# Modulation products inside the attentions, issued as two rounds of four matmuls

## The chip, the cores and the metric

The kernel runs on one core of a Trainium2 chip. The metric is the device time of one execution, in microseconds (us). Three runs of the kernel before gave 1478.65, 1478.90 and 1479.46, median 1478.9.

## The reference

Two trunk layers run over 128 context tokens and 256 latent tokens with a model width of 1024. A layer is: an adaptively modulated RMSNorm, one input projection, three parallel mixers (A: differential attention over 4 heads, B: pooling, C: windowed attention over 8 heads with a sink), a gated merge, an output projection, again a modulated norm, and a channel mixer (dense in layer 0, top-2-of-8 experts in layer 1).

What matters here is where the modulation comes from. `adaln_mods` computes six vectors per layer from a conditioning vector: `m = silu(c) @ w_ada[l] + b_ada[l]`, with `w_ada[l]` of 1024 x 6144. There are two conditioning vectors, one for latent and one for context tokens. So two rows are multiplied with 25 MB of weights a layer. The result is needed only at the norms and residuals of the rest of the layer and of the next, so the kernel computes it in pieces, placed among other work.

## The kernel before, in words

All 384 tokens are kept together as three blocks of 128. TensorE (PE) is the engine with the most work. Large products run in three passes of split operands (`mm3`, lines 766 to 768); the stages inside the attentions run as plain fp32 matmuls.

**The weights' path.** SyncE's queue (SP) loads every weight slot of 1 MB, as two transfers of 512 KB (`halves`, line 517), into a ring of three buffers (`raw`). Slot n goes to buffer n mod 3, and SP waits until the last user of that buffer is done. Slots that belong to `w_ada` need no splitting: PE reads `raw` itself, and when the product of a slot is complete PE raises `mm_done`, which lets SP refill the buffer.

**A modulation slot** covers 256 columns of `w_ada` and all 1024 rows (8 chunks k of 128). `ada_product` waits for both transfers of the slot, and then issues 8 matmuls with 32 stationary columns each. Matmul k goes to column group k mod 4 of the array and adds to the 32 PSUM partitions of that group in bank 7, so four matmuls can run beside each other, and a product is two rounds of four. The profile counts 2 instructions for a matmul: a product is 16 instructions of line 783, a round is 8.

**The attentions.** `attention(l, kind)` runs four times on PE: A and then C in layer 0 (phases 2 and 3), A and C in layer 1 (phases 4 and 5). Each walks 12 steps t, one for a head or a pair of heads (t // 3) and a block of queries (t % 3); block 0 has 128 keys, the others 384. In step t PE issues in this order, and PE keeps to its order:

- `scores(t + 2)`, the score matmuls of two steps ahead (line 1004), for t from 2 to 9;
- a modulation product, if t is in `ADA_STEPS`;
- `transposes(t)`, the turn of the weights (line 1022), which waits until VectorE (DVE) has combined the exponentials (`p_done`);
- `values(t - 1)` (line 1038), which waits for ScalarE's (ACT) copy of the turned weights.

For a step, the other engines do: DVE the maxima (line 2233), ACT two exponentials (line 1721), DVE the combination (lines 2244 or 2248), and, after the turn, ACT a copy to SBUF (line 1732). ACT's order is exps(t + 1), copy(t), with exps(11) behind copy(9). The DVE of attention C also has a sum of 1.75 us in step 5 (line 2288).

**Modulation slots.** The phases have 8, 7, 6 and 6 slots. Products 0 and 1 come ahead of step 0; the others stand in the steps named. When the attention begins, slots 0 to 2 are in the three buffers. Slot 3 can be loaded only when product 0 has been computed, slot 4 after product 1, slot 5 after product 2, and so on.

```
ADA_STEPS = {2: (1, 3, 5, 7, 9, 10), 3: (1, 4, 6, 8, 10),
             4: (1, 4, 6, 9), 5: (1, 4, 6, 9)}
for t in range(12):
    if t >= 2 and t + 2 < 12:
        scores(l, kind, t + 2)
    if t in ADA_STEPS[phase]:
        ada_product(phase, 2 + ADA_STEPS[phase].index(t))
    transposes(t)
    if t >= 1:
        values(t - 1)
```

Outside the attentions the same kind of product appears at line 793 (`gap_product`): one product alone, and later five in a row.

Of the kernel before, what the change touches and what calls it, by code (L numbers as in the profile page):

```python
# [15 lines left out]
KD = D // P  # L16
# [49 lines left out]
ADA_SLOTS = (8, 4, 8, 7, 6, 6)  # L66
# [10 lines left out]
EARLY_BUF = {0: 0, 1: 1, 2: 2, 3: 3, 4: 4, 5: 0, 7: 1, 9: 2}  # L77
EARLY = 5
GROUPS = ADA_SLOTS[0] // 2
ADA_STEPS = {2: (1, 3, 5, 7, 9, 10), 3: (1, 4, 6, 8, 10), 4: (1, 4, 6, 9), 5: (1, 4, 6, 9)}  # L80
assert all(2 + len(ADA_STEPS[p]) == ADA_SLOTS[p] <= 16 for p in ADA_STEPS)
SQS = (0, 1, 1 + N_HALF, 2 + N_HALF)
SQ0 = (0, BLK, BLK + 5 * N_HALF, BLK + 5 + 5 * N_HALF)
PROJ = ((0, 512), (512, 512), (2048, 512), (2560, 256), (1024, 512), (1536, 512))
# [55 lines left out]
def prefix_step_kernel(nc, a, outs, const):  # L140
    y_prompt, y_sample, new_dk, new_dv, new_wk, new_wv = outs
    ctx = ExitStack()
    with ctx:
# [12 lines left out]
        def sem(name):  # L156
            return ctx.enter_context(nc.semaphore(name))
# [162 lines left out]
        hi_done, lo_done, mm_done = sem("hi_done"), sem("lo_done"), sem("mm_done")  # L320
# [77 lines left out]
        def ada_slot(phase, i):  # L398

            if phase == 0:  # L400
                return FIRST_ADA[i]
            if phase == 1:
                return ADA_SLOTS[0] + 3 + RING * i
            l, kind = (phase - 2) // 2, (phase - 2) % 2
            return gate_slot(l, kind + 1, 0, 0) - ADA_SLOTS[phase] + i
# [17 lines left out]
        def ada_raw(n):  # L423

            return early[:, EARLY_BUF[n], :] if n in EARLY_BUF else raw[:, n % RING, :]
# [43 lines left out]
        def weight_col(t):  # L469

            return 1 + (T - P if t % 3 == 0 and t else 0)
# [24 lines left out]
        def raw_wait(eng, n, more=0):  # L496
            if n in EARLY_BUF:
                eng.wait_ge(side_in[EARLY_BUF[n]], early_wait(n))
            else:
                eng.wait_ge(raw_in[n % RING], more + 32 * raw_turn(n))  # L500
# [262 lines left out]
        def _(pe):  # L763
# [7 lines left out]

                return [w[:, n % RING, :].rearrange("p (k c) -> p k c", k=k) for w in (whi, wlo)]

            def ada_product(phase, i):

                n, last, bank = ada_slot(phase, i), ADA_SLOTS[phase] - 1, 7
                if phase == 0:
                    i, last = i % 2, 1
                raw_wait(pe, n)
                w = ada_raw(n).rearrange("p (k c) -> p k c", k=KD)  # L780
                for k in range(KD):
                    j = k % 4
                    mm = pe.matmul(ps[32 * j:32 * j + 32, bank, 0:256], sil32[:, k, 30 - 2 * i:62 - 2 * i], w[:, k, :],  # L783
                                   start=(i == 0 and k < 4), stop=(i == last and k >= 4), tile_position=(0, 32 * j))
                mm.then_inc(mm_done, 1)

            def gap_product(phase, i):
                last = GAP_SLOTS[phase] - 1
# [8 lines left out]
            def ada_pair(g):  # L797
                if g:
                    pe.wait_ge(ada_read, g)
                for i in range(2 * g, 2 * g + 2):  # L800
                    ada_product(0, i)

            def ada_end(phase, g=0):
                n = 2 * (GAP_SLOTS[phase] if phase in GAP_SLOTS else ADA_SLOTS[phase]) if phase else 4
                pe.wait_ge(ada_row, ada_turn(phase) if phase else g + 1)
                for c in range(2):
                    mm = pe.matmul(ps[:, 7, 256 + 32 * c:256 + 32 * c + n], adarow[:, c * P:(c + 1) * P], pick[:, 0:n],
                                   start=True, stop=True)
                mm.then_inc(ada_turned, 1)
# [52 lines left out]
            def first_units(products):  # L862
# [25 lines left out]
                for b in range(BLK):  # L888
                    if b == 2:
                        ada_product(0, 6)  # L890
                    mm = pair(K_A, 1, b)
                mm.then_inc(mm_done, 1)
                ada_product(0, 7)
                ada_end(0, 3)
                pe.wait_ge(lo_done, split_count(win_slot(0, 1) + 1))
# [97 lines left out]
            def scores(l, kind, t):  # L993

                h, qb = t // 3, t % 3
                if t >= 2:
                    pe.wait_ge(e_done, 24 * l + 12 * kind + t - 1)
                nk, k0 = (P, 0) if qb == 0 else (T, P)
                q, kk = (qTA, kTA[:, h, k0:k0 + nk]) if kind == 0 else (qTC, kTC[:, h // 2, k0:k0 + nk])
                for m in range(2):  # L1000
                    r = slice(64 * m, 64 * m + 64)
                    c0 = score_col(t) if kind else 0
                    out, lhs = ps[:, 2 * (t % 2) + m, c0:c0 + nk], q[r, h, qb * P:(qb + 1) * P]
                    mm = pe.matmul(out, lhs, kk[r], start=True, stop=True)  # L1004
                mm.then_inc(s_done, 1)

            def attention(l, kind):

                st0 = 24 * l + 12 * kind
                it0 = 24 * l + 12 * kind  # L1010
                phase = 2 + 2 * l + kind

                def transposes(t):
                    pe.wait_ge(p_done, st0 + t + 1)
                    if kind:
                        pe.wait_ge(pt_evac, it0 + t)
                    elif it0 + t >= 2:
                        pe.wait_ge(pt_evac, it0 + max(t - 1, 0))
                    k0 = kind * weight_col(t)
                    for m in range(1 + kind):  # L1020
                        for kb in range(1 if t % 3 == 0 else 3):
                            mm = pe.transpose(ps[:, 4 + (m if kind else t % 2), kb * P:(kb + 1) * P],  # L1022
                                              ebuf[:, t % 2, m, k0 + kb * P:k0 + (kb + 1) * P], ident)
                    mm.then_inc(tp_done, 1)

                def values(t):
                    h, qb = t // 3, t % 3
                    pe.wait_ge(pt_evac, it0 + t + 1)
                    grp = 8 * l + 4 * kind + h
                    if qb == 0 and grp >= 1:  # L1030
                        pe.wait_ge(o_evac, grp)
                    c = slice(h * P, (h + 1) * P) if kind == 0 else slice(512 + (h // 2) * 64, 576 + (h // 2) * 64)
                    keys = [vtok[:, 0, c]] if qb == 0 else [vtok[:, 1, c], vtok[:, 2, c], ctxv[:, c]]
                    for kb, v in enumerate(keys):
                        k = slice(kb * P, (kb + 1) * P)
                        for m in range(1 + kind):
                            rows, x = (slice(64 * m, 64 * m + 64), ptm[:, t % 2, m, k]) if kind else (slice(0, P), pt[:, t % 2, k])
                            mm = pe.matmul(ps[rows, 6, qb * P:(qb + 1) * P], v, x, start=(kb == 0),  # L1038
                                           stop=(kb == len(keys) - 1))
                    mm.then_inc(pv_done, 1)  # L1040

                scores(l, kind, 2)
                scores(l, kind, 3)
                pe.wait_ge(merge_top, 2 * l + kind + 1)
                ada_product(phase, 0)
                ada_product(phase, 1)
                if kind == 0:
                    pe.wait_ge(merge_done, 6 * l + 2)
                else:
                    pe.wait_ge(merge_read, 4 * l + 2)  # L1050
                for t in range(12):
                    if t >= 2 and t + 2 < 12:
                        scores(l, kind, t + 2)
                    if t in ADA_STEPS[phase]:
                        ada_product(phase, 2 + ADA_STEPS[phase].index(t))
                    transposes(t)
                    if t >= 1:
                        values(t - 1)
                    if t == 11 and kind == 1:
                        ada_end(phase)  # L1060
                values(11)
# [435 lines left out]
            for b in range(BLK):  # L1497
                pe.wait_ge(x_in[b], 16)
                for k in range(KD):
                    mm = pe.transpose(ps[:, 2 * b + k // 4, k % 4 * P:(k % 4 + 1) * P], xtok[:, b, k * P:(k + 1) * P], ident)  # L1500
                mm.then_inc(x_tr, 1)
                if b == 0:
                    pe.wait_ge(init_in, 16 * n_init)
                    for l in range(DEPTH):
                        n = R_END if l == 0 else R_C
                        mm = pe.transpose(ps[:, 6, l * P:l * P + n], vrows[0:n, l, :], ident[0:n, 0:n])
# [11 lines left out]
            for l in range(DEPTH):  # L1518
                if l:
                    mean_squares(2 * l)  # L1520
                input_projection(l)
                branch(l, 0)
                attention(l, 0)
                branch(l, 1)
                attention(l, 1)
                branch(l, 2)
                out_projection(l)
                if l == 0:
                    mean_squares(1)
                    units()  # L1530
                else:
                    router()
                    experts()
# [1240 lines left out]
```

## Time and profile before

| what | value |
|---|---|
| median of three runs | 1478.9 us |
| time of the profiled execution | 1479.42 us |
| span of the profiled execution | 1477.7 us |
| PE busy | 1445.6 us (98%) |
| DVE, ACT busy | 907.6 us (61%), 729.4 us (49%) |
| mean granted clock | 0.998 |
| attention A / C of layer 0 | 26.9 us / 32.1 us |
| attention A / C of layer 1 | 25.5 us / 31.3 us |

The span is from the first to the last instruction. The time is 1.7 us more than the span. The four attentions are 115.8 us of it together. The ends of matmuls in the trace are modelled, so the distance from one start to the next start is the safer measure of what a group of matmuls costs PE.

### The profile page before, as it was taken

What the parts mean: (1) busy time and instruction counts of PE and PEld (TensorE: products, weight loads), DVE (VectorE), ACT (ScalarE), POOL (GpSimd) and SP (SyncE); (2) the same over time, 40 slices, a digit from 0 to 9 for tenths busy, and PEclk for the clock granted to TensorE, in tenths of its full rate; (3) what the DMA queues carried; (4) which work ended last, traced back from release to release, by engine and by line L of the source; (5) the groups of instructions that cost most, each with busy time, mean ns of one, the idle gap of its engine ahead of it and who ended that gap; (6) DMA issues with size and microseconds to landing.
All of it is one profiled execution on the core that took longest, in us unless ns stands there. A gap on an engine that the chain in (4) does not pass through costs nothing.

```text
span 1477.7 us, 22390 instructions
## 1 busy us (share of the span) xinstructions
PE 1445.6 (98%) x8951; PEld 1276.5 (86%) x8951; DVE 907.6 (61%) x1081; ACT 729.4 (49%) x867; POOL 59.7 (4%) x59
## 2 busy tenths in 40 slices
PE   7999999999999999999999999999999999999997
PEld 5788969789999999998889879699888888888884
DVE  4543266555644345427532373737899999989888
ACT  4433354453433233225434262733478787787754
POOL 0100000000000000001000000001200000000030
PEclk9999999999999999999999999999999999999999
DMA  9844365468763355263532271645599999999991
GB/s 325 287 162 165 114 209 183 130 203 276 235 198 108 115 143 142 95 233 125 172 126 86 94 244 62 215 156 194 172 390 395 390 391 394 391 388 383 350 330 65
DMA packets 229146, 326.48 MB, mean 221 GB/s; under 512 B 8485, under 2 KB 154822, under 8 KB 228798
## 3 DMA queue, kind: packets, MB, share of 16 engines
q1 hardware_dynamic: 220160, 296.02, 58.7%
q0 software_dynamic: 6832, 25.88, 5.0%
q10 hardware_dynamic: 2062, 3.24, 0.6%
q8 instruction: 71, 1.16, 0.3%
q14 instruction: 21, 0.17, 0.0%
HBM read 310.14 MB, written 14.97 MB: 220 GB/s over the span
## 4 chain that ended last, share of the span: by engine, by line
PE 91%; DVE 4%; DMA 2%; ACT 1%; issue 1%; ACTq 0%; POOL 0%; DVEq 0%; SPq 0%; POOLq 0%
PE ps L766 26%; PE ps L768 25%; PE ps L767 25%; PE ps L783 2%; PE ps L1004 2%; PE ps L1038 1%; PE ps L1022 1%; DMA mrows<-g2d 1%; DMA raw<-in_w_ex_down_dram 1%; PE ps L859 1%; PE ps L1326 1%; PE ps L1286 1%; PE ps L983 0%; ACT ebuf L1721 0%; PE ps L793 0%
## 5 line engine op out<-in xcount | busy, mean ns | idle before, releaser
L766 PE MATMUL ps<-hhi,whi 128*128 128x384 f32 x824 | 277.0, 336 | 0.3 <-DVE hidlo L2659 0.3
L768 PE MATMUL ps<-hhi,wlo 128*128 128x384 f32 x824 | 275.7, 335 | 0.0
L767 PE MATMUL ps<-hlo,whi 128*128 128x384 f32 x824 | 275.7, 335 | 0.0
L2047 DVE TENSOR_TENSOR wlo<-raw,whi 128x2048 fp32r<-128x2048 f32 x65 | 148.7, 2289 | 173.7 <-ACT whi L1549 161.6
L766 PEld LDWEIGHTS ps<-hhi,whi 128*128 128x128 f32 x824 | 154.8, 188 | 2.6 <-issue 2.0
L767 PEld LDWEIGHTS ps<-hlo,whi 128*128 128x128 f32 x824 | 154.8, 188 | 0.3
L768 PEld LDWEIGHTS ps<-hhi,wlo 128*128 128x128 f32 x824 | 154.8, 188 | 0.0
L2538 DVE TENSOR_TENSOR wlo<-mraw,whi 128x2048 fp32r<-128x2048 f32 (+2 forms) x72 | 143.5, 1993 | 14.4 <-ACT whi L1818 14.0
L2538 DVE TENSOR_TENSOR wlo<-raw,whi 128x2048 fp32r<-128x2048 f32 (+2 forms) x72 | 144.3, 2019 | 11.9 <-ACT whi L1818 11.6
L1549 ACT ACTIVATE whi<-raw 128x2048 fp32r<-128x2048 f32 x60 | 114.6, 1912 | 74.0 <-PE ps L768 58.9
L1818 ACT ACTIVATE whi<-mraw 128x2048 fp32r<-128x2048 f32 (+2 forms) x72 | 120.9, 1679 | 57.1 <-PE ps L768 54.7
L766 PE MATMUL ps<-whi,xgh 128*128 128x512 f32 (+1 forms) x384 | 146.2, 381 | 0.3 <-DVE xgl L2527 0.3
L768 PE MATMUL ps<-whi,xgl 128*128 128x512 f32 (+1 forms) x384 | 142.9, 372 | 0.0
L767 PE MATMUL ps<-wlo,xgh 128*128 128x512 f32 (+1 forms) x384 | 142.9, 372 | 0.0
L1818 ACT ACTIVATE whi<-raw 128x2048 fp32r<-128x2048 f32 (+2 forms) x72 | 121.6, 1698 | 32.9 <-PE ps L768 24.6
L766 PE MATMUL ps<-whi,hhi 128*128 128x512 f32 (+1 forms) x285 | 108.9, 382 | 3.3 <-issue 2.0
L2645 DVE TENSOR_TENSOR wlo<-raw,whi 128x2048 fp32r<-128x2048 f32 (+1 forms) x35 | 73.8, 2109 | 57.9 <-ACT whi L1795 57.9
L768 PE MATMUL ps<-whi,hlo 128*128 128x512 f32 (+1 forms) x285 | 106.2, 372 | 0.0
L767 PE MATMUL ps<-wlo,hhi 128*128 128x512 f32 (+1 forms) x285 | 106.1, 372 | 0.0
L1795 ACT ACTIVATE whi<-raw 128x2048 fp32r<-128x2048 f32 (+1 forms) x36 | 63.8, 1771 | 54.4 <-PE ps L768 54.4
L766 PEld LDWEIGHTS ps<-whi,xgh 128*128 128x128 f32 x384 | 72.2, 188 | 12.5 <-issue 2.0
L768 PEld LDWEIGHTS ps<-whi,xgl 128*128 128x128 f32 x384 | 72.2, 188 | 10.2
(422 smaller groups left out, 2500.2 us busy)
## 6 DMA issues: line engine op xcount, KB each, us to landing
raw<-in_w_ada_dram SPq DMA_DIRECT2D x62, 512.0 KB, 5.3
raw<-in_w_gate_dram SPq DMA_DIRECT2D x48, 512.0 KB, 4.6
raw<-in_w_ex_up_dram SPq DMA_DIRECT2D x24, 1024.0 KB, 8.9
raw<-in_w_ex_down_dram SPq DMA_DIRECT2D x24, 1024.0 KB, 8.4
raw<-in_w_in_dram SPq DMA_DIRECT2D x43, 512.0 KB, 5.7
raw<-in_w_ex_gate_dram SPq DMA_DIRECT2D x16, 1024.0 KB, 8.1
mraw<-in_w_ex_gate_dram SPq DMA_DIRECT2D x16, 1024.0 KB
mraw<-in_w_ex_down_dram SPq DMA_DIRECT2D x16, 1024.0 KB, 9.4
```

Source lines behind the costliest of these rows:

```text
L766: pe.matmul(out, s[0], m[0], start=first, stop=False, **kw)
L767: pe.matmul(out, s[0], m[1], start=False, stop=False, **kw)
L768: return pe.matmul(out, s[1], m[0], start=False, stop=last, **kw)
L783: mm = pe.matmul(ps[32 * j:32 * j + 32, bank, 0:256], sil32[:, k, 30 - 2 * i:62 - 2 * i], w[:, k, :], start=(i == 0 and k < 4), stop=(i == ...
L859: mm = pe.transpose(ps[:, bank, b * P:(b + 1) * P], src, ident)
L1004: mm = pe.matmul(out, lhs, kk[r], start=True, stop=True)
L1549: act.activation(whi[:, n % RING, :], raw[:, n % RING, :], copy).then_inc(hi_done, 1)
L1795: act.activation(whi[:, s % RING, 0:used], raw[:, s % RING, 0:used], copy).then_inc(hi_done, 1)
L1818: act.activation(whi[:, m % RING, c:E_USED[m]], mraw[m % MRAW][:, c:E_USED[m]], copy).then_inc(hi_done, 1)
L2047: dve.tensor_tensor(wlo[:, n % RING, :], raw[:, n % RING, :], whi[:, n % RING, :].bitcast(F32), ALU.subtract).then_inc(lo_done, 1)
L2538: dve.tensor_tensor(wlo[:, m % RING, c:E_USED[m]], mraw[m % MRAW][:, c:E_USED[m]], whi[:, m % RING, c:E_USED[m]].bitcast(F32), ALU.subtrac ...
L2645: dve.tensor_tensor(wlo[:, s % RING, 0:used], raw[:, s % RING, 0:used], whi[:, s % RING, 0:used].bitcast(F32), ALU.subtract).then_inc(lo_d ...
```

## The change

`ada_product` gets an argument for the chunks k that it issues, and raises `mm_done` only with the last chunk. The table of steps is replaced by a table of halves: entry n of `ADA_HALVES[phase]` is the step in which half n is issued, and half n is round n % 2 of product 2 + n // 2. In every step the first half named stands where the product stood, ahead of the turn; a second one (only step 4 of phase 2) stands behind the turn. The wait for the slot's transfers is made before each half, and is for both transfers.

```diff
-ADA_STEPS = {2: (1, 3, 5, 7, 9, 10), 3: (1, 4, 6, 8, 10), 4: (1, 4, 6, 9), 5: (1, 4, 6, 9)}
+ADA_HALVES = {2: (0, 1, 2, 3, 4, 4, 5, 6, 7, 8, 9, 10), 3: (1, 2, 3, 4, 5, 6, 7, 8, 9, 10), 4: (1, 2, 4, 5, 6, 7, 9, 10), 5: (1, 2, 4, 5, 6, 7, 9, 10)}
...
-            def ada_product(phase, i):
+            def ada_product(phase, i, ks=range(KD)):
...
-                for k in range(KD):
+                for k in ks:
...
-                mm.then_inc(mm_done, 1)
+                if ks[-1] == KD - 1:
+                    mm.then_inc(mm_done, 1)
...
+                def ada_half(n):
+                    ada_product(phase, 2 + n // 2, range(4 * (n % 2), 4 * (n % 2) + 4))
...
-                    if t in ADA_STEPS[phase]:
-                        ada_product(phase, 2 + ADA_STEPS[phase].index(t))
+                    halves = [n for n, step in enumerate(ADA_HALVES[phase]) if step == t]
+                    if halves:
+                        ada_half(halves[0])
                     transposes(t)
+                    for n in halves[1:]:
+                        ada_half(n)
```

## Rows read from the trace of the kernel before

**Rows 1.** The page, part 4: shares of the chain that ended last, by engine.
```profile
PE 91%; DVE 4%; DMA 2%; ACT 1%; issue 1%; ACTq 0%; POOL 0%; DVEq 0%; SPq 0%; POOLq 0%
```

**Rows 2.** Busy time by stretch, the four attentions: stretch, length, engines, clock, DMA share, GB/s.
```profile
194.10:221.00 26.90, 26.38 (x254) 16.29 (x253) 19.52 (x46) 16.83 (x54) 0.00 (x0) 1.00 0.87 280
275.60:307.70 32.10, 30.58 (x325) 18.45 (x324) 21.85 (x50) 20.97 (x58) 0.00 (x0) 1.00 0.70 230
841.00:866.50 25.50, 24.53 (x220) 15.43 (x220) 19.52 (x46) 16.92 (x54) 0.00 (x0) 1.00 0.78 247
921.10:952.40 31.30, 29.72 (x310) 18.07 (x309) 22.05 (x51) 21.41 (x58) 0.00 (x0) 1.00 0.64 202
```

**Rows 3.** Timeline of PE, attention A of layer 0: start, us, engine, line, operation.
```profile
199.09 0.92 PE L1004 MATMUL ps<-kTA,qTA 64*128 64x384 f32 x4
200.05 0.55 PE L1022 MATMUL ps<-cst,ebuf 128*128 128x128 f32 x3
...
202.04 1.07 PE L783 MATMUL ps<-raw,sil 128*32 128x256 f32 x16
203.05 0.33 PE L1022 MATMUL ps<-cst,ebuf 128*128 128x128 f32 x1
...
204.40 0.55 PE L1022 MATMUL ps<-cst,ebuf 128*128 128x128 f32 x3
...
206.02 1.07 PE L783 MATMUL ps<-raw,sil 128*32 128x256 f32 x16
...
214.07 0.92 PE L1004 MATMUL ps<-kTA,qTA 64*128 64x384 f32 x4
214.92 1.07 PE L783 MATMUL ps<-raw,sil 128*32 128x256 f32 x16
215.92 0.33 PE L1022 MATMUL ps<-cst,ebuf 128*128 128x128 f32 x1
...
218.84 0.55 PE L1022 MATMUL ps<-cst,ebuf 128*128 128x128 f32 x3 [0.23 <-DVE ebuf L2244]
...
220.30 0.71 PE L1038 MATMUL ps<-pt,vtok 128*128 128x128 f32 x4 [0.24 <-ACT pt L1732]
...
220.99 0.42 PE L1095 MATMUL ps<-hhi,whi 128*128 128x384 f32 x1
```

**Rows 4.** Timeline of SP: second transfers of slots 3, 4 and 5, phase 2.
```profile
196.80 0.51 SPq L517 DMA_DIRECT2D raw<-in_w_ada_dram  x1
197.90 0.51 SPq L517 DMA_DIRECT2D raw<-in_w_ada_dram  x1
199.26 1.20 SPq L517 DMA_DIRECT2D raw<-in_w_ada_dram  x1
```

**Rows 5.** Line 517 by itself, the same three issues in order: time to landing.
```profile
DMA to landing us min/median/max: 4.6/4.6/4.6
...
DMA to landing us min/median/max: 8.0/8.0/8.0
...
DMA to landing us min/median/max: 9.6/9.6/9.6
```

**Rows 6.** The chain in order of time: one modulation product, then five in a row.
```profile
393.79 1.00 PE ps L793 x16
...
395.65 4.45 PE ps L793 x80
```

**Rows 7.** Timeline of ACT: the exponentials of step 11, phases 2 and 3.
```profile
216.46 0.57 ACT L1721 ACTIVATE ebuf<-ps,small 128x384 f32<-128x384 f32 x1
...
302.03 0.58 ACT L1721 ACTIVATE ebuf<-ps,small 128x385 f32<-128x385 f32 x1 [0.72 <-DVE small L2233]
```

**Rows 8.** Timeline of PE: waits for DVE in phases 3, 4 and 5.
```profile
289.73 0.87 PE L1022 MATMUL ps<-cst,ebuf 128*128 128x128 f32 x6 [0.63 <-DVE ebuf L2248]
...
864.72 0.55 PE L1022 MATMUL ps<-cst,ebuf 128*128 128x128 f32 x3 [0.73 <-DVE ebuf L2244]
...
935.28 0.87 PE L1022 MATMUL ps<-cst,ebuf 128*128 128x128 f32 x6 [0.62 <-DVE ebuf L2248]
```

More of the change, by code:

```diff
@@ L79 @@
 GROUPS = ADA_SLOTS[0] // 2
-ADA_STEPS = {2: (1, 3, 5, 7, 9, 10), 3: (1, 4, 6, 8, 10), 4: (1, 4, 6, 9), 5: (1, 4, 6, 9)}
-assert all(2 + len(ADA_STEPS[p]) == ADA_SLOTS[p] <= 16 for p in ADA_STEPS)
+ADA_HALVES = {2: (0, 1, 2, 3, 4, 4, 5, 6, 7, 8, 9, 10), 3: (1, 2, 3, 4, 5, 6, 7, 8, 9, 10), 4: (1, 2, 4, 5, 6, 7, 9, 10), 5: (1, 2, 4, 5, 6, 7, 9, 10)}
+assert all(4 + len(ADA_HALVES[p]) == 2 * ADA_SLOTS[p] <= 32 and max(ADA_HALVES[p]) < 11 for p in ADA_HALVES)
 SQS = (0, 1, 1 + N_HALF, 2 + N_HALF)
```

## The prediction

> **What bounds the kernel now.** I read the chain of waits first: PE holds 91% of it [rows 1], so anything that makes PE's own sequence longer or shorter shows in the time nearly one for one. Then the busy time by stretch, for the four attentions that the change touches. There PE is busy for 26.38 of 26.90, 30.58 of 32.10, 24.53 of 25.50 and 29.72 of 31.30 us [rows 2]. The idle time is the difference, 0.5 + 1.5 + 1.0 + 1.6 = 4.6 us. This is the most that a better filling of PE's waits could ever give, 0.3% of the time, and a change that only moves rounds can fill a part of it. The rest is small print: where the waits lie, what the rounds cost, and whether their weights are there. For the weights I read SP's timeline with its times to landing. In the first attention DMA is busy for 87% of the stretch at 280 GB/s [rows 2], so this is the one of the four in which weights can be late. The list of PE's waits names none between the attentions and up to the router, so what one gains or loses is not given back there.
>
> **The price of a round.** The number of matmuls stays the same. One product alone takes 1.00 us; five in a row take 4.45 [rows 6]. With p for a product and s for what a group costs once, p + s = 1.00 and 5p + s = 4.45, so p = 0.86 and s = 0.14. The product in step 3 agrees: 202.04 to 203.05, 1.01 us [rows 3]. A round that stands alone then costs 0.43 + 0.14 = 0.57 us and not 0.50. The groups inside the steps were 6, 5, 4 and 4 and become 12, 10, 8 and 8: 19 more, 19 x 0.14 = 2.6 us of PE time that was not there. From below, a group could cost nothing more (a round is 0.50 us, if s halves as well); from above 0.75 us, if s is paid on both sides of a round between two other kinds of matmul, where 0.14 was measured over runs of one kind. I take 0.57, the value of the nearest rows.
>
> The Trainium skill has a rule on this, in "TensorEngine Tiling (Array Packing)", Key Properties: a change of the tiling mode, and not merely of the tile, drains the engine. The trace's 0.14 us per group agrees with a drain. By that rule every added group is paid for, as I have it; without it the sum below would be some 1.5 us lower.
>
> **Phase 2, attention A of layer 0.** Here the halves stand in steps 0 to 10, two in step 4.
>
> *Slot 3.* Its first half moves from step 3 to step 2. The second transfer of slot 3 is issued at 196.80 and lands 4.6 us later, at 201.4 [rows 4, 5]. Neither can be earlier in the new order, since SP waits for product 0, which stays ahead of step 0. PE is ready for this half when scores(4) is out: 199.09 + 0.85 (the scores, as from 214.07 to 214.92) and some 0.1 for the group more in front, about 200.0 [rows 3]. So PE stands for 1.45 us, up to about 201.45 with the semaphore. Behind the wait are queued the turn of step 2 and the values of step 1. In the old order that product came at 202.04, with the weights 0.6 us old. The old wait for DVE before 200.05 (0.96 from 199.09, less 0.85: 0.12) disappears under it.
>
> *Slot 4.* Lands at 197.90 + 8.0 = 205.9 [rows 4, 5]. Up to the turn of step 4, old 204.40 [rows 3], the same four rounds have been done, in four groups for two: 204.40 + 1.45 + 0.27 - 0.12 = 206.0. Just not a wait.
>
> *Slot 5.* Lands at 199.26 + 9.6 = 208.86 [rows 4, 5]; its release by product 2, at the end of step 1, is unchanged. It is used in step 5. scores(7) was out at 206.02 [rows 3]. New: two rounds more than before (0.86), four more groups (0.54), the wait of 1.45, less 0.12 and a small one of 0.07: 208.7. A wait of 0.25. It may fall away: slot 6 is now issued some 1.4 us later, since product 3 ends later, and leaves slot 5 more of the bandwidth. I keep 0 and 0.25 as ends. Slots 6 and 7 come at about 3 us each behind slot 5 and are used later than that.
>
> *The end.* scores(11) was out at 214.92 [rows 3] with four products done inside the steps; now ten rounds are done by then. New: 214.92 + 0.86 + 6 x 0.135 + 1.45 + 0.25 - 0.19 = 218.1. From there the old chain was: product in step 9 (1.00), turn 9 at 215.92, exponentials of step 11 at 216.46, 0.54 later [rows 3, 7], turn 11 at 218.84, values 11 at 220.30, end at 220.99. With one round in step 9 the turn comes at 218.1 + 0.57, the exponentials 0.54 later at 219.2 (the maxima of step 11 are ready just then too), turn 11 is 2.38 later at 221.6, values(11) come 1.14 behind it (the old 1.46 less the wait for ACT that it held, 0.3), and last 0.69: 223.4. Against 220.99 this is +2.4, without the wait for slot 5 +2.2. I take **+2.3 us**. Had nothing been late, two rounds more ahead of scores(11) would still have cost 0.86 there and given back only 0.43 behind it.
>
> **Phase 3, attention C of layer 0.** Products 1, 4, 6, 8, 10 become rounds in 1 to 10. By step 5 the same four rounds are done in two more groups (+0.27). The turn of step 5, at 289.73, had waited some 0.69 us for DVE (from the scores' end; 0.63 by the row) [rows 8], behind DVE's sum; the round of step 5 now fills this wait, and DVE itself comes 0.1 later. So one round is done for nothing, and scores(11) comes 4 x 0.135 - 0.69 - 0.19 (a wait for ACT in step 8, filled) = 0.34 us earlier. The exponentials of step 11 were bound by the maxima [rows 7], hence by scores(11), and follow: **-0.35**. At worst 0, if DVE's sum moves with its scores.
>
> **Phases 4 and 5.** Rounds in 1, 2, 4, 5, 6, 7, 9, 10: every product keeps its step for the first round and puts the second off. No slot is needed earlier than before. In phase 4 scores(11) comes three groups later (+0.41) and gains 0.22 in small waits: +0.2. Behind it one round less in step 9 lets the exponentials go 0.3 earlier than they would, and the wait of 0.7 to 0.9 us before the turn at 864.72 [rows 8] takes up the round of step 10: **-0.1**. In phase 5 the wait of 0.69 before 935.28 [rows 8] is filled by the round of step 5, which pays for the four added groups and little more: **-0.1**. Each could be 0.4 better or 0.4 worse.
>
> **Sum.** 2.3 - 0.35 - 0.1 - 0.1 = +1.75 us. Against the profiled execution, 1479.42 (the span of 1477.7 and 1.7 around it), that is 1481.2. That execution lay 0.5 above the median of the runs, so against 1478.9 it is **1480.6**. A measurement of this kernel tells some 0.2%, 3.0 us, from no change, so my forecast is no measurable change, on the slow side. Its own range is 1479.7 to 1481.6.
>
> **Rivals.**
> - *The drain is dearer* (ends on the other side, slower). A round between two other kinds of matmul costs 0.75 us, s paid on both sides. Some two thirds of the 19 + 19 groups' 0.18 us lie on the path (the others fill waits): 38 x 0.18 x 0.6 = 4 us on top, 1484 to 1485. It decides from about 0.62 a round, where 38 x 0.05 x 0.6 brings the sum over +3.0. For it: rounds now touch scores on one side and the turn on the other in 38 places. Against: the product in step 3 sat so too and cost 1.01, which holds both sides already.
> - *The weights are there in step 2.* With less traffic beside it slot 3 lands at 200. Then phase 2 costs 0.85 and the sum is +0.3: 1479.2. Against: slot 3 is the first in the queue, and nothing ahead of it changes.
> - *The rounds fill the waits and cost nothing* (s halves with the round, and slot 3 is no wait): phase 2 +0.4, phase 3 -0.75, phases 4 and 5 -0.25 and -0.45, together -1.05: 1477.9. All of the 4.6 us would have to be won for 1474.3; the tails wait for ACT and DVE, whatever PE does, so that is out of reach.
>
> **How the numbers follow.** Forecast 0.64, dearer drain 0.12, weights there 0.12, waits filled 0.10, anything else 0.02. The range must hold 0.8: from 1478.6 (which takes in the second rival) to 1482.2 (the first steps of the dearer drain, and slots 4 and 5 later by some tenths). Slower by over 0.2% is 1481.9 and more: 0.12, nearly all from the dearer drain. Faster by over 0.2% is under 1475.9: 0.02. The same: 0.86.
>
> **What would show it.** In the timeline of PE: 8 instructions of line 783 from start to the next start in 0.57 us; a wait of about 1.4 us for the DMA of w_ada in step 2 of the first attention, and none elsewhere over 0.3; no wait before the turn of step 5 in layer 0's C and under 0.6 in layer 1's; the first attention longer by 2.3, the second shorter by 0.35. Rounds at 0.50 or over 0.62, a first attention no longer than 27.5 us, or a change in a stretch outside the attentions of over 0.5 us would make it wrong.

## The result

The changed kernel takes 1482.72 us (median of 15 runs, 1480.93 to 1485.59), the kernel before 1479.1 (15 runs on the same chip, 1477.87 to 1481.23). The ratio is 1.0023, with a 95% interval of 1.0016 to 1.0031: slower by 2.4 to 4.6 us. I had forecast 1480.6, within 1478.6 to 1482.2, and no measurable change with 0.86. The time is outside the range. The profiled execution took 1481.4 us with a span of 1479.7, 2.0 more than the profiled one of before.

The busy time by stretch, of the changed kernel, for the four attentions (stretch, length, PE, weight loads, DVE, ACT, POOL, clock, DMA share, GB/s). It answers to [rows 2]; the limits here are the first scores of an attention and the first gate product behind it.

```profile
193.91:223.18 29.27, 27.38 (x253) 15.76 (x253) 19.19 (x46) 16.69 (x54) 0.00 (x0) 1.00 0.84 268
277.77:309.60 31.83, 31.20 (x325) 17.93 (x324) 21.76 (x50) 20.96 (x58) 0.00 (x0) 1.00 0.72 227
842.87:868.95 26.08, 25.29 (x222) 15.04 (x221) 19.19 (x46) 16.81 (x54) 0.00 (x0) 1.00 0.70 220
923.54:954.80 31.26, 30.20 (x309) 17.62 (x309) 21.94 (x51) 21.52 (x58) 0.00 (x0) 1.00 0.63 203
```

Between the same two instructions the kernel before took 26.85, 32.13, 25.54 and 31.26 us. So the change is +2.42, -0.30, +0.54 and 0.00, in sum +2.66. The three stretches between the attentions are 54.59, 533.27 and 54.59 us in the one trace and 54.59, 533.29 and 54.59 in the other. So everything but the attentions agrees to 0.02 us between these two executions (to 0.06 us in the profiles of all kernels). An attention that no edit touched can differ by more: the first one, with the whole products of before, took 26.85 to 26.99 us in six profiles and 27.43 in a seventh (split_first, below, by late weights and a longer wait for ACT at its end). The +2.42 of the first attention is many times that; a difference of 0.2 us needs its rows to be believed.

The timeline of PE of the changed kernel, first attention (it answers to [rows 3]):

```profile
197.58 0.64 PE L783 MATMUL ps<-raw,sil 128*32 128x256 f32 x8
198.15 0.55 PE L1026 MATMUL ps<-cst,ebuf 128*128 128x128 f32 x3
...
199.14 0.92 PE L1005 MATMUL ps<-kTA,qTA 64*128 64x384 f32 x4 [0.22 <-ACT ebuf L1728]
201.28 0.64 PE L783 MATMUL ps<-raw,sil 128*32 128x256 f32 x8 [1.23 <-DMA raw<-in_w_ada_dram]
201.85 0.55 PE L1026 MATMUL ps<-cst,ebuf 128*128 128x128 f32 x3
...
205.77 0.64 PE L783 MATMUL ps<-raw,sil 128*32 128x256 f32 x8
206.34 0.55 PE L1026 MATMUL ps<-cst,ebuf 128*128 128x128 f32 x3
206.81 0.64 PE L783 MATMUL ps<-raw,sil 128*32 128x256 f32 x8
207.38 0.49 PE L1042 MATMUL ps<-pt,vtok 128*128 128x128 f32 x2
207.80 0.92 PE L1005 MATMUL ps<-kTA,qTA 64*128 64x384 f32 x4
208.65 0.64 PE L783 MATMUL ps<-raw,sil 128*32 128x256 f32 x8
...
217.81 0.64 PE L783 MATMUL ps<-raw,sil 128*32 128x256 f32 x8
218.38 0.33 PE L1026 MATMUL ps<-cst,ebuf 128*128 128x128 f32 x1
...
221.37 0.55 PE L1026 MATMUL ps<-cst,ebuf 128*128 128x128 f32 x3 [0.43 <-DVE ebuf L2251]
```

What to see in it: a round is 0.57 us from its start to the next start (205.77 to 206.34, 208.65 to the next start at 209.22), which is half a product's 0.86 and the 0.14 of a group. The round of step 2 waits for its weights (the row at 201.28). The wait in the row at 199.14 is also new: scores(4) now wait for ACT, which I had not foreseen. Scores(11) are out at 217.81, 3.1 us later than before (23.90 for 20.78 from the attention's start), and the end comes 0.7 us nearer to them than it was.

SP's timeline of the changed kernel, the second transfer of slot 3 (it answers to [rows 4]):

```profile
196.57 0.51 SPq L517 DMA_DIRECT2D raw<-in_w_ada_dram  x1
```

Line 517 by itself, the same issue, its time to landing (it answers to [rows 5]):

```profile
DMA to landing us min/median/max: 4.7/4.7/4.7
```

It lands at 201.27, and the round starts at 201.28. PE was through with scores(4) at 199.99, so the wait is 1.29 us by starts.

### The profile page after: what moved, and what is told of

It is laid out like the page before. It is cut to its first block, busy times and chain, and to the rows that moved or that the text cites. A ratio compares the mean times of both kernels' runs of the same rounds, so it can differ in the third digit from the quotient of the medians.

```text
span 1479.7 us, 22390 instructions
## 1 busy us (share of the span) xinstructions
PE 1450.4 (98%) x8951; PEld 1276.9 (86%) x8951; DVE 906.8 (61%) x1081; ACT 729.1 (49%) x867; POOL 59.7 (4%) x59
## 4 chain that ended last, share of the span: by engine, by line
PE 92%; DVE 3%; DMA 3%; issue 1%; ACT 1%; SPq 0%; POOL 0%; DVEq 0%; ACTq 0%; POOLq 0%
PE ps L766 26%; PE ps L768 25%; PE ps L767 25%; PE ps L783 2%; PE ps L1005 2%; PE ps L1042 2%; PE ps L1026 1%; DMA mrows<-g2d 1%; DMA early<-in_w_ada_dram 1%; DMA raw<-in_w_ex_down_dram 1%; PE ps L860 1%; PE ps L1333 1%; PE ps L1293 0%; PE ps L984 0%; PE ps L794 0%
## 5 line engine op out<-in xcount | busy, mean ns | idle before, releaser
L2240 DVE TENSOR_REDUCE small<-ps 128x2 f32<-128x768 f32 (+3 forms) x48 | 37.0, 778 | 73.8 <-PE ps L1005 73.3
```

The lines of the kernel that those rows point to most:

```text
L2240: dve.tensor_reduce(small[:, p, 0:2], ps[:, 2 * p:2 * p + 2, c], X, ALU.max, negate=True).then_inc(nmax_done, 1)
```

## The experiments

In the short diffs, `ADA_PLAN` is my table: for a phase and a step, the halves ahead of the turn and those behind it. Halves 2i and 2i + 1 side by side are a whole product. Where a table is not shown, the phase has the whole products of before.

**One attention alone, and the other three.** The first kernel:

```diff
+2: rounds of the changed kernel, steps (0, 1, 2, 3, 4, 4, 5, ..., 10)
+3, 4, 5: whole products in the steps of before
```

> Only attention A of layer 0 (phase 2) has its products as separate rounds; the other three attentions are as before. Theory 1 (the change's cost is a wait for the weights of slot 3 plus the price of added groups, both in this attention): this attention, from its first scores to the first gate product behind it, takes 29.2 to 29.4 us against 26.85, the other three stay within 0.1 us of 32.13, 25.54 and 31.26, and the time is 2.2 to 2.6 us over before (ratio 1.0015 to 1.0018), with the wide spread of the changed kernel's runs if the wait for the weights is what spreads them. Theory 2 (the loss is spread over all four): under 1.5 us over before.

Measured: 29.30, 32.14, 25.52 and 31.27 us. Ratio 1.0020, interval 1.0011 to 1.0029, median 1482.21 against 1479.04. The second kernel is the reverse (phase 2 as before, 3 to 5 with rounds):

> Attention A of layer 0 is as before; only the other three (phases 3 to 5) have rounds. Theory 1: they take 31.8, 26.1 and 31.3 us against 32.13, 25.54 and 31.26, in sum +0.2, the time is within 0.5 us of before and the runs spread as little as those of before. Theory 2: over 1.5 us over before, or a time that moves where no attention does.

Measured: 26.85, 31.83, 26.09 and 31.25 us, sum +0.24. Ratio 1.0001, interval 0.9992 to 1.0010. So each attention takes the same to 0.03 us whether the others are changed or not, and nearly all of the loss is the first one's. The median of first_only, 3.2 over before, was more than the 2.2 to 2.6 expected, though 1.6 to 4.3 is its interval.

**Less to load for slot 3.**

```diff
+if (phase, i) == (2, 3):
+    halves(n, [d[:, 0:1], d[:, 4:5]], [s[:, 0:1], s[:, 4:5]])
+    continue
```

> The changed kernel, but slot 3 of attention A of layer 0 loads only chunks 0 and 4 of its 8 (two transfers of 128 KB for two of 512 KB); the rest of that product reads what the buffer held, so part of the modulation is not computed. If the late weights hold PE in step 2: the wait before that round falls from 1.2 us to under 0.3, slots 4 and 5 come about 2 us earlier too, and this attention takes 27.7 to 28.1 us, 1.2 to 1.5 less than the changed kernel's 29.27. If something else holds it (drain, turn, scores): it stays at 29.0 or more.

Measured: 27.98 us for the first attention, 1.29 less than the changed kernel's and 1.13 over before, ratio 1.0012 (1.0003 to 1.0021). The timeline of PE of this kernel:

```profile
199.26 0.92 PE L1014 MATMUL ps<-kTA,qTA 64*128 64x384 f32 x4 [0.22 <-ACT ebuf L1737]
200.11 0.64 PE L792 MATMUL ps<-raw,sil 128*32 128x256 f32 x8
200.68 0.55 PE L1035 MATMUL ps<-cst,ebuf 128*128 128x128 f32 x3
```

The round stands right behind the scores, with no wait left. So 1.3 of the 2.4 us are the late weights, and 1.1 are the two rounds that now stand ahead of scores(11), the price of the added groups and the wait for ACT, less what the shorter tail gives back.

**The changed kernel again.**

> The changed kernel once more, beside the others on one chip. Theory 1: attentions of 29.3, 31.8, 26.1 and 31.3 us, the sum 2.6 us over before, and 2 to 4 us over before in the time. If the profiled execution is one of the longer ones, its trace shows where the runs of the changed kernel differ by up to 4 us: in the wait for slot 3 (theory 1), or outside the attentions (theory 2).

Measured: 29.57, 31.83, 26.08 and 31.25 us; median 1481.9, 2.9 over the 1479.04 of before, ratio 1.0021 (1.0012 to 1.0030). So the same kernel, measured again, lay 2.9 over where it had lain 3.6 over. Its profiled execution was one of the longer ones (span 1482.0), and shows where the difference lies: from the last attention to the end it took 526.9 us, against 524.9 in the first profile of the same kernel. The busy time by stretch of this execution, in the router, behind DVE's selection:

```profile
1046.50:1051.50 5.00, 2.98 (x27) 2.79 (x25) 4.86 (x7) 2.73 (x4) 3.37 (x2) 1.00 0.00 0
1051.50:1054.50 3.00, 2.97 (x15) 2.97 (x16) 2.70 (x8) 1.25 (x2) 0.00 (x0) 0.56 0.00 0
1054.50:1059.50 5.00, 5.00 (x29) 5.00 (x29) 4.45 (x26) 0.00 (x0) 0.00 (x0) 0.58 0.65 262
```

The granted clock (third column from the end) is 1.00 while PE waits 2.05 us for the selection, and then 0.56 and 0.58, about the lower level of 1.2 GHz for most of 8 us. The matmuls behind it are then on the path: from the selection's end to the side slots' product (line 1268) it was 14.1 us, against 12.5 with a clock of 0.70 and 0.84 in the first profile, and 11.8 in the kernel before with 1.00. So the router's clock can cost up to 2.4 us of an execution. That is the far end. Over the 14 profiles of kernels with this wait, the stretch took 11.8 to 12.1 us with a clock of 1.00 (six profiles), 12.5 in six of the eight with the low clock, and 14.1 and 14.2 in the other two. Whether the fall belongs to the change was the question of the next experiments.

The Trainium skill, in "TensorE: Matmul & The Clock Gate", What's actually happening, has the throttled clock as the state at rest, which PE's activity lifts; the wait of 2.05 us ahead of the fall agrees with that. That the same wait brings it in one execution and not in another, as the last two profiles below show, is what its remark on a window that runs free of the kernel would give (Part 1); no run here shows that window.

**A pure delay.**

```diff
+if (l, o) == (0, 1):
+    for _ in range(11):
+        pe.matmul(out[:, 0:P], ident, ident, start=True, stop=True)
```

> The kernel before, with 11 matmuls of 128x128 that nobody reads put at the start of the branch behind attention A of layer 0: 11 x 0.22 = 2.4 us of PE time, and no other edit. Theory 1 (what the attentions gain and lose explains 2.66 of the 2.9 to 3.6 us by which the median moved; the rest is the clock, which the traces show at 0.5 to 0.7 in the router behind DVE's selection in four executions that came there 2 us later, and at 1.00 in the two that did not): the router of this kernel shows the low clock as well, the time is 2.9 to 3.6 over before and the runs spread up to 6 us over. Theory 2 (the rest is chance, or belongs to the rounds themselves): 2.2 to 2.6 over, and a clock of 1.00 in the router.

Measured: 29.31 us for the first attention (the extra matmuls stand at its end), 2.46 over before, the others within 0.02, a clock of 1.00 in the router, and a time only 1.5 over before (ratio 1.0008, 0.9999 to 1.0017). Both theories missed. That a late arrival at the router brings the low clock is not borne out by this kernel. It is one profile, and PE's wait for the selection was 1.48 us in it, where it was 2.0 to 2.5 in the others, so it doesn't settle the question either. Its part behind the attentions was the shortest of all, 524.0 us. The router's clock is not all that moves that part: it took 525.3 us in the first profile of the kernel before, also with a clock of 1.00.

**No idle PE in the router.**

```diff
-                keep_warm(6, 12)
+                keep_warm(6, 22)
```

> The changed kernel, with 22 for 12 idle-time matmuls ahead of the router's wait for the selection, where PE stood for 2.0 to 2.5 us. Theory 1: PE is not idle there any more, the clock stays at 1.00 through the router, and the time is that of the attentions alone, 2.3 to 2.7 over before, with runs that lie within 1.5 us of each other. Theory 2: the clock or the spread don't change, 2.9 to 3.6 over.

Measured: attentions as in the changed kernel (29.26, 31.83, 26.08, 31.26), median 1481.4 against 1478.7, ratio 1.0016 (1.0007 to 1.0025). The runs lie within 1480.03 and 1481.97, where the changed kernel's reached 1485.59. The busy time by stretch in this kernel's router:

```profile
1045.50:1050.50 5.00, 5.00 (x48) 5.00 (x46) 4.83 (x8) 2.66 (x4) 3.23 (x2) 1.00 0.00 0
1050.50:1053.50 3.00, 2.96 (x27) 2.80 (x26) 2.96 (x8) 1.25 (x2) 0.00 (x0) 1.00 0.00 0
1053.50:1058.50 5.00, 5.00 (x46) 5.00 (x47) 4.42 (x28) 0.60 (x1) 0.00 (x0) 1.00 0.75 296
```

PE is busy for 5.00 of 5 us ahead of the selection, and the clock holds. The same edit in both kernels, on one chip:

> The kernel before with 22 for 12 idle-time matmuls ahead of the router's wait for the selection. Theory 1 (the attentions alone make the difference; the router's clock adds to it in some executions): clock 1.00 in the router, time 0 to 0.4 under before, and the changed kernel with the same edit lies 2.3 to 2.9 over this one. Theory 2 (something beside the attentions costs the changed kernel 1 us): the difference of the two is 3.3 or more.

> The changed kernel with the same edit, again, to stand beside it on one chip. Theory 1: 2.3 to 2.9 us over the one above. Theory 2: 3.3 or more.

Measured: 1478.49 and 1481.36, 2.9 us apart in the medians; against their common runs of before the ratios are 0.9998 (0.9989 to 1.0007) and 1.0014 (1.0005 to 1.0023). Attentions of 26.99, 32.13, 25.75, 31.27 and of 29.69, 31.83, 26.08, 31.26, +2.7 in these two executions. With the clock at 1.00 in both, the two kernels differ by what the attentions differ. The medians cannot exclude half a microsecond more.

The record also has the mean clock of every single execution, with three digits: for the changed kernel in the two sets of runs that it had, and for the kernel before in three sets that ran beside experiments. At 0.998 and above, the changed kernel's median is 1481.5 us (8 of its 26 executions) and that of the kernel before 1478.8 (43 of 98): 2.7 apart, as the attentions are. Below 0.997 they are 1483.7 (7 of 26) and 1480.4 (16 of 98). So low clocks go with long executions in both kernels. That they are more frequent in the changed one, 7 of 26 against 16 of 98, is not shown by so few; and its longest execution, 1485.59, had 0.998, so something else spreads its runs too.

**The second round behind the turn.**

```diff
+2: {1: ((0,), (1,)), 3: ((2,), (3,)), ..., 10: ((10,), (11,))}   # 3, 4, 5 alike
```

> Every product keeps its old step, but its second round comes behind the turn of that step, not ahead of it: 21 more groups, and the weights needed in the same steps as before. Theory 1 (a group costs 0.14 us, and the wait of the first attention is for weights): the first attention has no wait for weights over 0.2; a round takes 0.57 from start to next start; turns come 0.43 us earlier, which shortens the tails a little, so of 21 x 0.14 = 2.9 us some 1.5 to 2.5 stay: attentions together 1.0 to 2.3 us over before. If a group costs nothing: under 0.5 over before.

Measured: 28.13, 32.58, 26.61 and 31.57 us, sum +3.1, more than the 1.0 to 2.3 expected; ratio 1.0024 (1.0015 to 1.0033). No wait for weights. The timeline of PE of this kernel, last attention A, step 9:

```profile
863.48 0.64 PE L786 MATMUL ps<-raw,sil 128*32 128x256 f32 x8
864.04 0.33 PE L1029 MATMUL ps<-cst,ebuf 128*128 128x128 f32 x1
864.30 0.64 PE L786 MATMUL ps<-raw,sil 128*32 128x256 f32 x8
864.87 0.71 PE L1045 MATMUL ps<-pt,vtok 128*128 128x128 f32 x4
```

The round behind the turn also costs 0.57, and the turn ahead of it takes 0.26 for the 0.17 that it takes ahead of values. So a group behind the turn is 0.23 us in an attention A, not 0.14. In an attention C it is 0.14. The timeline of PE of this kernel, attention C of layer 0, step 4, and then the same turn ahead of values in the kernel placed, whose experiment is below:

```profile
288.25 0.88 PE L1029 MATMUL ps<-cst,ebuf 128*128 128x128 f32 x6 [0.23 <-DVE ebuf L2258]
289.06 0.64 PE L786 MATMUL ps<-raw,sil 128*32 128x256 f32 x8
```

```profile
286.60 0.87 PE L1029 MATMUL ps<-cst,ebuf 128*128 128x128 f32 x6 [0.23 <-DVE ebuf L2258]
287.41 0.44 PE L1045 MATMUL ps<-ptm,vtok 128*64 128x128 f32 x4
```

The turn takes 0.81 us in either place. The values of C are matmuls with 64 columns (128*64 in the row), those of A have 128 columns like the turn (128*128): where turn and values are of one form, a round between them costs more than where they are of two. The table splits 19 products, so it adds 19 groups, and not the 21 that I had expected: 10 in the A attentions and 9 in the C, 10 x 0.23 + 9 x 0.14 = 3.6 us. The sum of +3.1 is 0.5 less; the likely reason, by subtraction and not by a row, is that some of it fell into waits. This shows the price of a group without any late weights.

**What the last attention A lost it by.** The changed kernel lost 0.54 there and I had forecast a gain of 0.1. The timeline of PE of the kernel before, scores(11) and what follows, and then scores(11) of the changed kernel (18.95 and 19.86 us from the attention's start, 0.91 later):

```profile
859.94 0.92 PE L1004 MATMUL ps<-kTA,qTA 64*128 64x384 f32 x4
860.79 1.07 PE L783 MATMUL ps<-raw,sil 128*32 128x256 f32 x16
```

```profile
862.73 0.92 PE L1005 MATMUL ps<-kTA,qTA 64*128 64x384 f32 x4
```

Two kernels with only this attention changed, one profile each:

```diff
+whole_first, 4: {1: ((0, 1), ()), 4: ((2,), ()), 5: ((3,), ()), ..., 10: ((7,), ())}
+split_first, 4: {1: ((0,), ()), 2: ((1,), ()), 4: ((2, 3), ()), 6: ((4, 5), ()), 9: ((6, 7), ())}
```

> Only A of layer 1 is changed: rounds in 4, 5, 6, 7, 9, 10, but product 2 whole in step 1. Theory 1 (halving the product of step 1 lets the scores of step 4 run into the exponentials of step 2, so that its second round in step 2 is all added): no wait of the first scores of the loop for ACT, and 25.5 to 25.7 us, 0.4 to 0.6 less than the changed kernel's 26.08. Theory 2 (the loss is in the later rounds): 26.0 or more.

> Only A of layer 1 is changed: product 2 as rounds in steps 1 and 2, all others whole in their old steps. Theory 1: the wait for ACT of 0.2 us and 25.9 to 26.1 us against 25.54. Theory 2: 25.4 to 25.7.

Measured: 25.77 and 25.83 us, +0.23 and +0.29, and the changed kernel's +0.54 is nearly their sum. Neither theory had it right: both parts lose. The differences are small, and the same attention untouched was once 25.75 (warm_before, where its slot 3 landed late); no wait for weights stands in the last attention A of either trace. Timelines of PE, split_first and then whole_first:

```profile
845.73 0.39 PE L1045 MATMUL ps<-pt,vtok 128*128 128x128 f32 x2
846.34 0.92 PE L1008 MATMUL ps<-kTA,qTA 64*128 64x384 f32 x4 [0.22 <-ACT ebuf L1731]
```

```profile
849.77 0.64 PE L786 MATMUL ps<-raw,sil 128*32 128x256 f32 x8
850.52 0.55 PE L1029 MATMUL ps<-cst,ebuf 128*128 128x128 f32 x3
851.08 0.46 PE L1045 MATMUL ps<-pt,vtok 128*128 128x128 f32 x2
851.47 0.92 PE L1008 MATMUL ps<-kTA,qTA 64*128 64x384 f32 x4
```

In the first, the halved product of step 1 lets PE reach scores(4) 0.43 us earlier, but these may overwrite their bank only when ACT has finished the exponentials of step 2, and 0.29 of the 0.43 go into that wait (by starts 846.05 to 846.34, 0.22 by the row); the put-off round costs 0.57 in step 2, where the old order had a wait of only 0.12 to fill. In the second, the halved product of step 4 brings the turn to DVE's combination 0.18 us too early (850.34 to 850.52), and the values that follow to 0.18 more (850.90 to 851.08). The whole product had hidden both.

**Rounds only where a wait was.** First by the waits of the trace of before, with rounds in the C attentions' steps 4 and 5 and in all tails:

```diff
+2: {..., 9: ((8,), ()), 10: ((9,), (10,)), 11: ((11,), ())}
+3: {1: ((0, 1), ()), 4: ((2,), ()), 5: ((3,), ()), 6: ((4, 5), ()), 8: ((6,), ()), 9: ((7,), ()), 10: ((8, 9), ())}
+4: {..., 9: ((6,), ()), 10: ((7,), ())}
+5: {1: ((0, 1), ()), 4: ((2,), ()), 5: ((3,), ()), 6: ((4, 5), ()), 9: ((6,), ()), 10: ((7,), ())}
```

> Whole products in the steps of before, save where a round falls into a wait that the trace of before shows: in step 5 of both attentions C (DVE's sum), and in steps 9 to 11 at the ends of the attentions. Theory 1: 0.4 us less in attention C of either layer, 0.3 to 0.6 less in A, 1.4 to 2.0 us less in all four together; the time 1.0 to 2.5 under before (with a start earlier in the router the clock need not fall). Theory 2 (rounds cost what they fill): within 0.3 us of before in every attention.

Measured: 26.73, 31.99, 26.37 and 31.27 us, median 1478.33 against 1478.7, ratio 0.9994 (0.9985 to 1.0003). The gains are 0.12 and 0.14 in layer 0, a third of those expected, and none in the last attention; the third attention was 0.83 longer, by a wait that is not the plan's. The timeline of PE of this kernel, and the time to landing of slot 3's second transfer, issued at 842.70:

```profile
850.53 1.07 PE L786 MATMUL ps<-raw,sil 128*32 128x256 f32 x16 [1.17 <-DMA raw<-in_w_ada_dram]
```

```profile
DMA to landing us min/median/max: 7.8/7.8/7.8
```

In the kernel before the same transfer took 6.6 us and landed just when its product was due; in two more profiles of that kernel it took 5.8 and 5.7. A transfer that lands with nothing to spare in one execution can be a wait in the next. Then with fewer groups, and with the idle-time matmuls:

```diff
+2: {..., 9: ((8,), ()), 10: ((9,), ()), 11: ((10, 11), ())}
+3: {1: ((0, 1), ()), 4: ((2,), ()), 5: ((3,), ()), 6: ((4, 5), ()), 8: ((6, 7), ()), 10: ((8, 9), ())}
+4: {..., 9: ((6,), ()), 10: ((7,), ())}
+5: {1: ((0, 1), ()), 4: ((2,), ()), 5: ((3,), ()), 6: ((4, 5), ()), 9: ((6, 7), ())}
```

> Whole products in the old steps, with rounds only where the traces showed a wait: A of layer 0 has product 6 as rounds in steps 9 and 10 and product 7 whole in step 11; both C have their second product as rounds in steps 4 and 5; A of layer 1 has its last product as rounds in steps 9 and 10. Groups added: 4. By waits and 0.14 a group: 26.3, 31.7, 25.2 and 30.85 us for 26.85, 32.13, 25.54 and 31.26, together 1.7 less; the time 1.2 to 2.0 under before. If rounds in waits gain nothing: within 0.4 of before. If slot 3 of A in layer 1 lands late, as in one trace, that attention is 26.4.

> The same with 22 for 12 idle-time matmuls in the router. Theory 1: a clock of 1.00 there, and 1.4 to 2.4 us under before.

Measured: 26.77, 32.14, 25.15, 31.28 (placed) and 26.81, 32.14, 25.14, 31.28; medians 1478.41 and 1478.26 against 1479.27, ratios 0.9996 (0.9987 to 1.0005) and 0.9998 (0.9989 to 1.0007). Only the tail of the third attention came out as reckoned (-0.39 for -0.35). The round in DVE's wait of step 5 gained nothing by itself, in either C attention: the trace then has two waits of 0.2 us for DVE, in steps 4 and 5, where it had one of 0.6. The timeline of PE, attention C of layer 0, from step 5 on, of placed and then of the changed kernel:

```profile
288.62 0.64 PE L786 MATMUL ps<-raw,sil 128*32 128x256 f32 x8
289.46 0.88 PE L1029 MATMUL ps<-cst,ebuf 128*128 128x128 f32 x6 [0.20 <-DVE ebuf L2258]
```

```profile
291.54 0.64 PE L783 MATMUL ps<-raw,sil 128*32 128x256 f32 x8
292.11 0.88 PE L1026 MATMUL ps<-cst,ebuf 128*128 128x128 f32 x6
```

From the attention's start the turn of step 5 comes at 14.15 us in the kernel before, 14.15 in placed and 14.34 in the changed kernel. In the first two PE waits for DVE there, and has done four rounds by then: placed had only put off a round from step 4, and DVE was no earlier for it. The changed kernel had brought one forward and has done five, for 0.2 us more. That fifth round is what it gains and placed doesn't.

Neither kernel is measurably faster than the one before. The clock in the router was 0.77 and 0.80 in placed, 1.00 in placed_warm.

**The kernel before, profiled twice more.**

> The kernel before, one more profile. If the low clock in the router belongs to any kernel with an idle PE ahead of the selection, and not to the change: it can show here (seven of ten kernels without the extra idle-time matmuls had it), and the part behind the attentions is then 0.7 us or more longer than with a clock of 1.00. If it belongs to the change, it is 1.00.

> The kernel before, a further profile, with the same expectations as the last: a low clock in the router in one of the two or both if any kernel can have it.

Measured: attentions of 26.92, 32.13, 25.51, 31.27 and 26.85, 32.12, 25.52, 31.28. The busy time by stretch in the router, of look1 and then of look2:

```profile
1043.70:1048.70 5.00, 2.80 (x26) 2.61 (x24) 4.86 (x7) 2.55 (x4) 3.39 (x2) 1.00 0.00 0
1048.70:1051.70 3.00, 2.94 (x24) 2.75 (x24) 2.93 (x9) 1.25 (x2) 0.00 (x0) 1.00 0.00 0
1051.70:1056.70 5.00, 4.97 (x44) 5.00 (x45) 4.45 (x26) 0.60 (x1) 0.00 (x0) 1.00 0.71 285
```

```profile
1043.80:1048.80 5.00, 2.54 (x24) 2.35 (x22) 4.86 (x7) 2.28 (x3) 3.34 (x2) 1.00 0.00 0
1048.80:1051.80 3.00, 3.00 (x22) 3.00 (x23) 2.93 (x9) 1.25 (x2) 0.00 (x0) 0.83 0.00 0
1051.80:1056.80 5.00, 5.00 (x37) 5.00 (x36) 4.42 (x27) 0.60 (x1) 0.00 (x0) 0.76 0.72 289
```

The kernel before has the low clock too, in one execution and not in the next, with the same code and nearly the same times of arrival. So it is not the change's. The part behind the attentions took 524.4 us in look1 and 525.0 in look2, 0.6 apart where 0.7 or more was expected. Of 14 profiles without the extra idle-time matmuls 8 had the low clock; of four with them none had.

## Why the prediction was wrong, point by point

- *PE bounds the attentions, and nothing between them gives anything back*: right. The stretches between agree to 0.02 us in the first two profiles.
- *A lone round costs 0.57 us*: right, in the timeline of every kernel with rounds. The dearer drain (0.75; by its own terms, s on both sides, it should have been 0.43 + 0.28 = 0.71) is refuted for rounds ahead of the turn; behind it, in an attention A, a group does cost 0.23 and not 0.14 (behind). The count was off by one: the round of step 0 follows products 0 and 1 directly and adds no group, so there are 18 more groups and not 19.
- *Phase 2, +2.3*: measured +2.42 and +2.45 (after, first_only). The wait for slot 3 was forecast as 1.45 us up to 201.45 and was 1.29, up to 201.28, with a wait of 0.29 for ACT just ahead of it that I did not have; small3 took the 1.29 away. That slot 4 and slot 5 would be no wait or one of at most 0.25: right, none in the first profile and some 0.1 us each in the second (again). That scores(11) then came 3.13 later, with 3.18 forecast, is in part luck: the wait for ACT made up for most of the 0.25 of slot 5 and the 0.14 of the group in step 0, neither of which came. The rival of weights that are there in time is out; with them there the attention still cost 1.13 (small3), where that rival had 0.85.
- *Phase 3, -0.35*: measured -0.30, with scores(11) 0.29 earlier, where I had 0.34. Right. But it isn't the round in step 5 that gains: placed had one there too and gained nothing. It gains where the rounds ahead of it have been brought forward, so that the fifth round stands in the wait and not the fourth.
- *Phase 4, -0.1*: measured +0.54. This is the term of the sum that failed, and it failed in kind. Scores(11) was to come 0.2 later and the rest to give 0.3 back; scores(11) came 0.91 later and the rest gave 0.38 back. I counted every small wait of the old order as one that a round would fill, and had no new wait behind a product that became shorter. The two kernels with parts of it show such waits, for ACT (0.29 us) and for DVE with the values behind it (0.18 twice), and add up to it.
- *Phase 5, -0.1*: measured 0.00. Within what I had allowed. The round in step 5 did not fill DVE's wait here: as in placed it was put off and not brought forward, and two waits of 0.2 us stood for one of 0.6.
- *The sum, +1.75*: the attentions gave +2.66. The missing 0.9 is 0.64 of phase 4, 0.12, 0.05 and 0.1 of the others. The upper ends that I had given for the parts (2.4, 0, 0.3 and 0.3) come to 3.0 and would have held 2.66; I added up the middles and narrowed the range about their sum.
- *From the sum to the time*: this step failed too, and it is what carried the time out of the range. With the +2.66 of the attentions alone it would have been 1481.6, within 1478.6 to 1482.2. I had let the time follow the attentions one for one and put whatever else differs between executions at nothing. The medians of the first comparison were 3.6 us apart (the ratio says 3.4), and 2.66 lies in its interval of 2.4 to 4.6. So of the 1.6 us by which the ratio exceeds my forecast 0.9 are the attentions, and for the other 0.7 no profile accounts. What bears on it: the same kernel measured again was 2.9 over; with the router's clock held, the two kernels were 2.9 apart; in executions with a mean clock of 0.998 and above, 2.7. Chance among 15 executions and the router's clock, which I had left out and which can move an execution by up to 2.4 us, are the likely sources. That the clock falls more often in the changed kernel was not shown, and the cause of this part stays open. The kernel with a pure delay (+2.5 in its trace, +1.5 in its time) says that the medians themselves are uncertain by about 1 us.
- *The chances*: 0.12 on slower than 0.2% was too low with a forecast of +1.75 and a threshold of +3.0. The rival that I gave for this side was the drain; the right ones would have been new waits behind shortened products, and a spread of the executions that no stretch of the attentions shows.

## What to carry to other kernels

Before a product is moved to an earlier step, set its slot's landing beside the new place; the issue may be bound to a release that does not move, as here, and then all the earliness becomes a wait. And a product cut in two to fill a wait must be charged twice: for the 0.14 us of the added group, and for the waits that the whole one had hidden where it stood; walk through the semaphores of the next instruction, not only of the one that is to be filled. A wait is filled to profit with work brought forward. Work put off into it gains only where what then runs earlier is what the wait is for: at the end of the last attention A (placed, -0.39 us), but not in steps 4 and 5 of the C attentions, where DVE came no earlier. Where a change is worth some tenths of a microsecond and the runs spread over 2 us, compare stretch by stretch between fixed instructions first, and let the median only confirm.

## What the runs showed of the hardware

Behind a PE wait of 2.0 to 2.5 us in the router the granted clock fell to 0.56 to 0.84 in the stretches of 3 and 5 us that follow, in 8 of 13 profiles, and stayed at 1.00 in the other 5, one and the same kernel showing both. A fourteenth profile, with a wait of 1.5 us (delay), stayed at 1.00. Ten more matmuls in the wait kept it at 1.00 in four of four. A transfer of 512 KB at one place of the kernel, slot 3's second in the attention A of layer 1, took between 4.7 and 7.8 us to land in ten profiles, and 5.7 to 6.6 in three of the same kernel. A group of matmuls with 32 columns, put in by itself, cost 0.14 us between scores and turn and between a turn and values of 64 columns, and 0.23 us between a turn and values of 128 columns.
